# Sums of squares for five norms: the vector engine adds chunk pairs, the tensor engine sums the total and the newest pair

## The reference

```python
# first block
h = rmsnorm(x, g_mix) * (1 + sc1) + sh1
x = x + (1 + gt1) * mixer(h, ...)            # ends in  merged @ w_o
h = rmsnorm(x, g_ffn) * (1 + sc2) + sh2      # norm 1
x = x + (1 + gt2) * conv_ffn(h, ...)         # ends in  (silu(a) * b) @ w_down
x = rmsnorm(x, g_final)                      # norm 2
# second block
hn = rms_norm(x, norm_mix_g_2)               # norm 3
h = x + conformer_conv(hn, ...)              # pw1, GLU, depthwise, layer_norm, silu, pw2
h = h + sq_relu_mlp(rms_norm(h, norm_ffn_g_2), ffn_w_up_2, ffn_w_down_2)   # norm 5
return rms_norm(h, final_norm_g_2)           # norm 6

def rmsnorm(x, g):
    return x * rsqrt(mean(x * x, axis=-1) + EPS) * g
```

## Time and profile before

| | us |
|---|---|
| timed runs, median of 3 | 2769.27 (2768.43 to 2769.63) |
| profiled execution | 2764.23 |
| its span, first to last instruction | 2762.4 |
| TensorE busy | 2641.9 (96%) |
| VectorE busy | 1939.0 (70%) |
| ScalarE busy | 1209.4 (44%) |

### The profile page before, as it was taken

One profiled execution on the slowest core, in us unless ns is written; L12 is line 12 of the kernel. 1 busy time (PEld: TensorE's weight loads), 2 busy tenths in 40 slices (PEclk: granted clock), 3 DMA queues, 4 the chain that ended last, 5 costly groups with the idle time before them and its releaser, 6 DMA issues.

```text
span 2762.4 us, 39657 instructions
## 1 busy us (share of the span) xinstructions
PE 2641.9 (96%) x14749; PEld 2298.8 (83%) x14749; DVE 1939.0 (70%) x2742; ACT 1209.4 (44%) x1559; POOL 101.7 (4%) x145
## 2 busy tenths in 40 slices
PE   3499999999998999999999999998999999999998
PEld 2488888888887888888888888886888888888886
DVE  6977778886887888855666547998676644566444
ACT  1244644444554655544555541004454434444443
POOL 0011111100000000000000000000000000000000
PEclk8599999999999999999999999999999999999998
DMA  8898777765776777755565545552556655666553
GB/s 317 294 304 259 221 238 244 244 201 159 227 250 223 235 248 245 230 188 186 184 188 186 179 139 147 153 153 75 190 178 189 190 190 186 188 184 188 183 183 107
DMA packets 492579, 557.32 MB, mean 202 GB/s; under 512 B 18854, under 2 KB 458279, under 8 KB 492199
## 3 DMA queue, kind: packets, MB, share of 16 engines
q1 hardware_dynamic: 474023, 488.50, 55.3%
q0 software_dynamic: 18432, 67.12, 7.9%
HBM read 553.45 MB, written 2.10 MB: 201 GB/s over the span
## 4 chain that ended last, share of the span: by engine, by line
PE 93%; DVE 4%; issue 2%; SPq 1%; ACT 1%; DMA 0%; DVEq 0%; ACTq 0%
PE ps L1374 53%; PE ps L1375 27%; PE ps L1655 8%; PE ms L1413 2%; DVE norm_rows L901 1%; DVE wlo L820 1%; PE ms L1422 1%; PE ms L1680 0%; DMA att<-in_x 0%; DVE tCDE L901 0%; PE ms L1513 0%; SPq L380 0%; DVE norm_rows L843 0%; PE ms L1665 0%; PE ms L1447 0%
## 5 line engine op out<-in xcount | busy, mean ns | idle before, releaser
L1374 PE MATMUL ps<-xhl,whi 128*128 128x512 f32 (+1 forms) x4368 | 1554.8, 401 | 23.0 <-DVE xhl L865 16.7
L820 DVE TENSOR_TENSOR wlo<-raw,whi 128x1024 fp32r<-128x1024 f32 x794 | 971.2, 1224 | 673.0 <-ACT whi L505 665.6
L505 ACT CAST whi<-raw 128x1024 fp32r<-128x1024 f32 x794 | 831.0, 1049 | 1174.4 <-PE ps L1375 1100.4
L1375 PE MATMUL ps<-xhl,wlo 128*128 128x256 f32 (+1 forms) x4368 | 1224.5, 280 | 0.0
L1374 PEld LDWEIGHTS ps<-xhl,whi 128*128 128x128 f32 (+1 forms) x4368 | 823.5, 189 | 227.1 <-issue 29.8
L1375 PEld LDWEIGHTS ps<-xhl,wlo 128*128 128x128 f32 (+1 forms) x4368 | 827.0, 189 | 3.3 <-issue 2.9
L1374 PE MATMUL ps<-ghl,whi 128*128 128x512 f32 x1024 | 360.9, 395 | 0.0
L1375 PE MATMUL ps<-ghl,wlo 128*128 128x256 f32 x1024 | 289.5, 283 | 0.0
L1374 PE MATMUL ps<-fhl,whi 128*128 128x512 f32 x704 | 248.7, 395 | 0.0
L1374 PEld LDWEIGHTS ps<-ghl,whi 128*128 128x128 f32 x1024 | 192.3, 188 | 44.3
L1655 PE MATMUL ps<-xg,raw 128*128 128x256 f32 x1024 | 221.3, 379 | 0.0
(11 more groups left out here) (221 smaller groups left out, 1555.9 us busy)
## 6 DMA issues: line engine op xcount, KB each, us to landing
raw<-in_w_in SPq DMA_DIRECT2D x176, 512.0 KB, 4.2
raw<-in_w_up SPq DMA_DIRECT2D x176, 512.0 KB, 3.7
ada<-in_w_ada POOLq DMA_DIRECT2D x128, 512.0 KB, 4.5
raw<-in_ffn_w_up SPq DMA_DIRECT2D x128, 512.0 KB, 3.7
raw<-in_ffn_w_down SPq DMA_DIRECT2D x128, 512.0 KB, 3.3
raw<-in_conv_w_pw SPq DMA_DIRECT2D x96, 512.0 KB, 3.7
raw<-in_w_down SPq DMA_DIRECT2D x88, 512.0 KB, 3.3
att<-in_w_ada SPq DMA_DIRECT2D x32, 1024.0 KB, 7.2
```

The lines of the kernel that those rows point to most:

```text
L505: nc.scalar.copy(whi[t % SPL][:, :, :], raw[t % RAW][:, :, :]).then_inc(s_hi, 1)
L820: nc.vector.tensor_tensor(wlo[t % SPL][:, :, :], raw[t % RAW][:, :, :], whi[t % SPL][:, :, :].bitcast(F32), ALU.subtract).then_inc(s_lo, 1)
L1374: mm(o, h, x, start=start, stop=stop, skip_group_check=True)
L1375: return mm(o[:, 0, :], l, x[:, 0, :], start=False, stop=stop, skip_group_check=True)
```

## The change

Squares of the first pair go into a tile `older`, those of every later pair into `newest`. VectorE adds `newest` to `older` for pairs 1 to 6 (`add_older`), and ScalarE may write the next pair only after that. When the last pair is there, TensorE sums `older` (`older_sum`) and `newest` (`newest_sum`) with two matmuls each. The two tiles are the halves of `sq`; the gained squares of norm 3 get two tiles of their own. `root` waits for the new semaphore `s_var2`. The first norm and the layer norm keep `statistic`.

Core of the diff (the same steps in the other stages are left out where they read alike):

```diff
-            def square_gained(n, i):
-                act.wait_ge(s_acc, n - 1)
+            def new_square(r, j):
+                if j > 1:
+                    act.wait_ge(s_old, 6 * r + j - 1)
+                nc.scalar.activation(newest if j else older, res[:, 2 * j:2 * j + 2, :], ACT.Square).then_inc(s_new, 1)
+            def new_square_gained(j):
+                if j > 1:
+                    act.wait_ge(s_oldg, j - 1)
...
+            def add_older(r, j):
+                if 1 <= j <= 6:
+                    dve.wait_ge(s_new, 8 * r + j + 1)
+                    if j > 1:
+                        dve.wait_ge(s_old, 6 * r + j - 1)
+                    nc.vector.tensor_tensor(older, older, newest, ALU.add).then_inc(s_old, 1)
+            def add_older_gained(j):
...
# VectorE, WO, and the same way in the other stages
                     split_lo(0, t + q)
+                    if q == 6:
+                        add_older(0, j - 1)
...
# VectorE, second DOWN
+                    if u and t > n and t % n == 4:
+                        add_older(1, t // n - 1)
+                        add_older_gained(t // n - 1)
...
# VectorE, PW2
+                    if q == 3:
+                        add_older(2, j - 1)
                     if j == 7 and q < 4:
                         gained_lo(range(4 * (q - 1), 4 * q))
...
# VectorE, second DN2
+                    if half and t > 8 and t % 8 == 4:
+                        add_older(3, t // 8 - 1)
...
# TensorE
+            def older_sum(r):
+                pe.wait_ge(s_old, 6 * (r + 1))
+                for m in range(2):
+                    mm(bank_o[:, 0:T], ones[:, :], older[:, m, :], start=m == 0, stop=False)
+            def newest_sum(r):
+                pe.wait_ge(s_new, 8 * (r + 1))
+                for m in range(2):
+                    ins = mm(bank_o[:, 0:T], ones[:, :], newest[:, m, :], start=False, stop=m == 1)
+                ins.then_inc(s_var2, 1)
...
# WO
+                    if j == 7 and q == 3:
+                        older_sum(0)
...
-                if j:
-                    statistic(8, (j - 1,))
             modulation(0, ADA_START + M_UP // 8 - 1)
-            statistic(8, (7,))
+            newest_sum(0)
...
# second DOWN: nothing between the groups; PW1, after its second unit
-                    if u and j:
-                        second_block_statistics(j - 1)
-                            second_block_statistics(7)
+                            second_block_statistics()
...
+            def second_block_statistics():
+                older_sum(1)
+                newest_sum(1)
+                pe.wait_ge(s_newg, 8)
+                pe.wait_ge(s_oldg, 6)
+                for i, x in enumerate((older_g, newest_g)):
+                    for m in range(2):
+                        ins = mm(bank_f[:, 0:T], ones[:, :], x[:, m, :], start=i + m == 0, stop=i + m == 2)
...
# PW2 and the first UP2
-                if j:
-                    statistic(40, (j - 1,))
-                    up2(0, 0, lambda q: statistic(40, (7,)) if q == 1 else None)
+                    up2(0, 0, lambda q: (older_sum, newest_sum)[q](2) if q < 2 else None)
...
# second DN2
-                    if half and j:
-                        statistic(48, (j - 1,))
-            statistic(48, (7,))
+            older_sum(3)
+            newest_sum(3)
```

More of the change, by code:

```diff
@@ L190, in build @@
         sq = sb("sq", [P, 4, T])
+        newest, older = sq[:, 0:2, :], sq[:, 2:4, :]
         mixer = ExitStack()
@@ L223, in build @@
         cb = sb("cb", [P, PC, T], F32, ffn)
+        newest_g, older_g = (sb(f"gained_squares{i}", [P, 2, T], F32, ffn) for i in range(2))
         ffn.close()
@@ L649, in _ @@
                     act.wait_ge(s_free[(G_WO + j - 1) % 2], free_at(G_WO + j - 1))
-                    square(8 + j - 1, j - 1)
+                    new_square(0, j - 1)
                 if j < 7:
@@ L658, in _ @@
             act.wait_ge(s_free[(G_WO + 7) % 2], free_at(G_WO + 7))
-            square(8 + 7, 7)
+            new_square(0, 7)
             root(1)
@@ L739, in _ @@
                 act.wait_ge(s_xc, i // 2 + 1)
-                square(32 + i, i, ucv)
+                square(8 + i, i, ucv)
             root(4)
@@ L768, in _ @@
             gained_hi(range(12, 16))
-            square(40 + 7, 7)
+            new_square(2, 7)
             def up2(i, half):
@@ L829, in summed, with root @@
                 return nc.vector.tensor_tensor(part[G % 2][:, :, :], ps[G % 2][:, :, 0, :], part[G % 2][:, :, :], ALU.add)
-            def root(n, eps, used, var=bank_o[:, 0:T], after=None):
-                dve.wait_ge(s_acc, used)
+            def add_older(r, j):
[5 more added lines that the diff above has]
+            def add_older_gained(j):
+                if 1 <= j <= 6:
+                    dve.wait_ge(s_newg, j + 1)
+                    if j > 1:
+                        dve.wait_ge(s_oldg, j - 1)
+                    nc.vector.tensor_tensor(older_g[:, :, :], older_g[:, :, :], newest_g[:, :, :], ALU.add).then_inc(s_oldg, 1)
+            def root(n, eps, ready, used, var=bank_o[:, 0:T], after=None):
+                dve.wait_ge(ready, used)
                 if after is not None:
@@ L936, in _ @@
                 split_lo(0, t)
-            root(0, EPS1, 8)
+            root(0, EPS1, s_acc, 8)
             norm_split(0, 0, H_QKV, lambda c: gmod[:, 0, c:c + 1], lambda c: mod[:, c:c + 1])
@@ L1286, in _ @@
             split_lo(0, T_PW2 + 1)
-            root(4, EPS2, 40)
+            root(4, EPS2, s_acc, 16)
             def scaled(c):
@@ L1347, in _ @@
                     split_lo(0, T_UP2[half] + 5)
-                    root(5, EPS2, 48)
+                    root(5, EPS2, s_var2, 4)
                 with dve.Fori(0, 8) as i:
@@ L1405, in group, with statistic @@
                         each(q)
-            def statistic(n0, steps, total=8, o=bank_o[:, 0:T], apart=1):
-                for i in steps:
-                    n = n0 + apart * i
+            def statistic(n0):
+                for i in range(8):
+                    n = n0 + i
                     pe.wait_ge(s_sq, n + 1)
                     for m in range(2):
-                        ins = mm(o, ones[:, :], sq[:, 2 * (n % 2) + m, :], start=i == 0 and m == 0, stop=i == total - 1 and m == 1)
+                        ins = mm(bank_o[:, 0:T], ones[:, :], sq[:, 2 * (n % 2) + m, :], start=i == 0 and m == 0, stop=i == 7 and m == 1)
                     ins.then_inc(s_acc, 1)
+            def older_sum(r):
[7 more added lines that the diff above has]
+                ins.then_inc(s_var2, 1)
             def modulation(g, group, sums=None):
@@ L1449, in _ @@
             pe.wait_ge(s_ang, 1)
-            statistic(0, range(8))
+            statistic(0)
             with pe.Fori(0, ADA_START // 2) as i:
@@ L1684, in _ @@
             ins.then_inc(s_mean, 1)
-            statistic(32, range(8))
+            statistic(8)
             for j in range(8):
                 group(0, 0, T_PW2 + 4 * j, G_PW2 + j, from_x(H_PW2 if j == 0 else None))
-                if j:
-                    statistic(40, (j - 1,))
             def up2(i, half, each=None):
```

33 lines of the change are left out of this document (18 added, 15 removed).

## The result

| | before, us | changed, us | difference |
|---|---|---|---|
| first timing, medians of 4 and 4 | 2769.45 | 2737.68 | -31.8; ratio 0.9886 (95%: 0.9868 to 0.9903) |
| second timing, 15 and 5 | 2765.92 | 2745.39 | -20.5; ratio 0.9915 (0.9901 to 0.9929) |
| third timing, 9 and 4 | 2767.57 | 2740.75 | -26.8; ratio 0.9901 (0.9886 to 0.9916) |
| means of all executions, 43 and 15 | 2767.8 (2762.1 to 2775.0) | 2741.1 (2736.4 to 2745.8) | -26.7, plus or minus 1.9 |

The change makes the kernel about 1% faster. The ratios are those of the record, which are not quotients of the two medians (in the second timing these would give 0.9926, the means 0.9915). Pooled, the gain is 26.7 us where 25 were forecast. The plus or minus is twice the standard error from the two spreads, 2.9 and 3.3 us.

The account below looks back on a forecast made before the run. TensorE was taken to set the pace in these stages. Removed matmuls (-25.6 us) plus PW2's add (0.65) made about -25 us, from 2769.27 to 2744.3 us; range 2740.5 to 2750.5 us.

Parts of the forecast that it names:

- Removed matmuls: Five norms, 60 matmuls fewer: each statistic taken from between product groups gains its full time, together 25.6 us.
- WO and PW2: Six statistics leave the chain in each of these two stages, 6 x 0.85 = 5.1 us gained in each.
- The sign in the prediction: In traces of the changed kernel, a WO and a PW2 group should have a period of 11.3 us.
- The backlog of PW2: In PW2's group 7 the sixth add delays the last square, so TensorE waits 0.65 us longer.
- Cover elsewhere: VectorE's adds in WO, the last DOWN stage, DN2 and PW2's groups 2 to 6 cost zero.
- the new waits: ScalarE's squares and VectorE's adds wait for each other from the third pair on; both partners are early.
- Rivals 1: VectorE does not keep up in WO (4.1 us) and PW2 loses 0.7 us more: 2749.1 us; chance 0.11.
- 3: All 30 adds end up on the path in every stage: 5 us gained, 2764.3 us; chance 0.03.
- 4: The removed matmuls were hidden, so only PW2's add is left: 2769.9 us; chance 0.02.
- 5: Exchanges between squares and adds become the pace: 13.4 us slower, 2782.7 us; chance 0.02.
- From the profiled execution to the timed ones: For the whole kernel, the timed median's 5 us above the profiled execution was carried over to the changed kernel.
- rival 2: TensorE's clock at stage ends shifts, 2.5 us either way: 2741.8 or 2746.8 us; chance 0.10 beyond 1.5 us.

Follow-up runs that it names:

- wo_extra2: Changed kernel with two all-ones float32 matmuls of 128x256 put back once, behind the second group of WO; a single execution took 2740.7 us.

## Why the prediction was right and wrong

**Removed matmuls.** Right: a statistic costs its full time, 0.85 to 0.86 us. DN2 gave 5.09 us (forecast 5.1), the last DOWN 10.3 (10.3). Putting one, two or four such matmuls back cost 0.43, 0.86 and 1.73 us beside the pace.

**WO and PW2.** This is the term of the sum that failed: 5.1 us for each. I took the period without a statistic from the earlier trace rows, a group of 11.31 us in a stretch that ran at the slower pace, and subtracted it from 12.16. That gave 0.85, the statistic's own time. But without statistics these groups can run at 11.09 us, and then a statistic costs 1.07 us: 0.86 of its own and 0.21 for the slower pace behind it. WO gave 5.58 instead of 5.1, since its groups g2 and g3 also became faster; from g4's modulation sum on they are slow in both kernels. PW2 gave 6.4 instead of 5.1, in one trace of five 5.0. Together that is 1.8 us more than the forecast. The sign in the prediction that WO's and PW2's period would be 11.3 us failed in the same way. One look at a second group in the trace of before would have shown 11.09: WO's own first step without a statistic, between the read-outs at 798.13 and 809.22, already did.

```profile
798.13 0.58 ACT L513 COPY part<-ps 128x512 f32<-128x512 f32 x1
809.22 0.58 ACT L513 COPY part<-ps 128x512 f32<-128x512 f32 x1
821.39 0.58 ACT L513 COPY part<-ps 128x512 f32<-128x512 f32 x1
```

**The backlog of PW2.** Right in place and cause. 0.65 us was forecast; the step from PW2 to UP2 grew by 0.75 us, of which 0.58 to 0.6 are the add and the rest is PW2's faster pace, which the forecast did not have. TensorE's wait, forecast at about 1.0 us, was 1.16 or 1.17 us in four traces and 0.93 in the one with the slower PW2.

**Cover elsewhere, and the new waits.** Right. The adds cost nothing in WO, DOWN and DN2, as cutting them short showed. Between the groups ScalarE's squares waited for nothing: in the changed kernel's trace the idle time before them is at the ends of three stages, for the residual and not for an add. Rivals 1, 3, 4 and 5 did not come.

**From the profiled execution to the timed ones.** This is the other step that failed. I carried the 5 us between the profiled execution of before and the median of three over to the changed kernel, as if it were a fixed offset, and widened the range only by "a little" for the spread. It is chance. 43 executions of before lie between 2762.1 and 2775.0 us. The stages' sum gives 26.6 us, so against the pooled mean of before the changed kernel belongs at 2741.2 us, and its 15 executions have the mean 2741.1. The four executions of the first timing were 2736.4 to 2740.0, low draws beside four high ones of before, 2768.4 to 2771.3.

The forecast was 2744.3 us and the first timing 2737.68, 6.6 us less. Of this 1.5 us are the three executions of before that stood above their kernel's mean, 1.7 us the stages' sum (26.6 instead of 24.95, the pace in WO and PW2), and 3.5 us the chance of four low executions. The range reached only 3.8 us below the forecast, and of these just 1.3 us (from 2741.8 to 2740.5) were for the spread of runs, which is what the range had wrong. None of the three parts alone would have put the time outside, and the pooled mean of 2741.1 us lies inside, so the miss is in part bad luck.

**The clock, rival 2.** It acts, at other places than the one priced (the end of WO, 2.5 us either way): 1.5 to 1.7 us at the start of the diagonal matmuls and 1.5 us at the layer norm's sums. It moves from trace to trace in both kernels. Whether the change makes it likelier stays open.

What stays open: why the pace has two levels, why the first step of PW2 and of the first UP2 takes now the one and now the other, and why DOWN and DN2 have only one. For groups of four units the runs show what sets the pace (two wide float32 matmuls between groups: slower; four: faster), the second in one trace at each place, and not through which mechanism.

## What to carry to other kernels

A matmul between the products of an engine that is never idle costs its time, and 0.7 us of work on a half-idle engine in its place costs nothing, except where that engine has a backlog before a stage's end: look for the add's place there first. When a period with an operation is compared with one without, take more than one reference period: the pace itself may depend on the operation. And before a forecast of 25 us gets a range, find out by how much one execution differs from the next; three timed runs within 1.2 us of each other said nothing about a spread of 13.

## What the runs showed of the hardware

- Groups of the same products run at two steady paces with TensorE busy all the time and the granted clock at 1.00: 11.09 or 11.31 us for 32 pairs (347 or 353 ns a pair). The pace holds over whole loops. Groups of five and eight units ran at 2.81 us a unit in every trace.
- Two float32 matmuls of 128x256 between groups left the slower pace wherever the start was known to be the faster one (g2 of WO, PW2 of before, wo_extra2). Four left the faster one in all four places tried, each in one trace. Four of one column changed it in WO and in the first UP loop, both ways, and did nothing at two other places.
- The clock after a wait of 3.16 us: 1.00 in one trace, 0.50 for the first stretch in the other, at the same place of the program. After a wait of 2.44 us: 1.00 in one trace, 0.58 in another.
- An all-ones float32 matmul of 128x256 took 0.43 us on the path, one of 128x1 about 0.22 us (0.90 us for four ahead of a loop).
